# Differential attention: the product with the values between the wide and the narrow scores on TensorE

## What is computed

```
def attend(q, k, v):
    s = einsum('cbhqd,cbhkd->cbhqk', q, k)      # c = 0, 1; d = 64
    p = softmax(s, axis=-1)
    a = p[0] - lam_val * p[1]
    return einsum('bhqk,bhkv->bhqv', a, v)      # v has 128 columns
```

## Time and profile before

| | us |
|---|---|
| three runs, median (lowest, highest) | 4268.17 (4264.69, 4269.55) |
| span of the profiled execution, first to last instruction | 4263.6 |
| PE busy in it | 3903.4 (92%) |
| DVE busy | 2098.1 (49%) |
| ACT busy | 1607.7 (38%) |
| POOL busy | 562.6 (13%) |
| PE share of the chain that ended last | 77% |

### The profile page before, as it was taken

One profiled execution on the slowest core, in us unless ns is written; L12 is line 12 of the kernel. 1 busy time (PEld: TensorE's weight loads), 2 busy tenths in 40 slices (PEclk: granted clock), 3 DMA queues, 4 the chain that ended last, 5 costly groups with the idle time before them and its releaser, 6 DMA issues.

```text
span 4263.6 us, 67437 instructions
## 1 busy us (share of the span) xinstructions
PE 3903.4 (92%) x28266; PEld 3208.1 (75%) x28266; DVE 2098.1 (49%) x3022; ACT 1607.7 (38%) x2639; POOL 562.6 (13%) x628
## 2 busy tenths in 40 slices
PE   6988897878999998988899989999999998899999
PEld 4866686766888776756688766677888887678887
DVE  3545454656221353267523664454655427655564
ACT  3333333333111233155322335644334336554333
POOL 0035303642000001002100000000220003000220
PEclk8988898888999999999899999999999999999999
DMA  5234433131221122101233230131223330322232
GB/s 155 82 130 144 149 97 115 35 100 50 70 70 60 55 71 69 60 11 57 94 98 99 79 85 21 42 129 51 91 97 99 95 108 15 112 79 77 93 103 85
DMA packets 248534, 355.08 MB, mean 83 GB/s; under 512 B 9299, under 2 KB 158502, under 8 KB 247846
## 3 DMA queue, kind: packets, MB, share of 16 engines
q1 hardware_dynamic: 233840, 300.49, 21.9%
q0 software_dynamic: 13840, 50.11, 3.7%
q10 hardware_dynamic: 550, 0.17, 0.0%
HBM read 336.50 MB, written 14.24 MB: 82 GB/s over the span
## 4 chain that ended last, share of the span: by engine, by line
PE 77%; DVE 12%; ACT 7%; issue 2%; POOL 2%; DMA 1%; ACTq 0%; DVEq 0%; SPq 0%; POOLq 0%
PE psum L233 20%; PE psum L234 20%; PE psum L235 20%; PE psum L230 14%; ACT arena L341 3%; DVE arena L264 3%; PE psum L239 3%; DVE arena L274 2%; DVE rw L264 2%; DVE rx L335 2%; ACT arena L345 1%; POOL arena L379 1%; DVE arena L278 1%; ACT rw L345 1%; DVE arena L270 1%
## 5 line engine op out<-in xcount | busy, mean ns | idle before, releaser
L233 PE MATMUL psum<-rx,rw 128*128 128x512 f32 (+2 forms) x2864 | 1047.0, 366 | 54.9 <-DVE rx L335 28.8
L234 PE MATMUL psum<-rx,rw 128*128 128x512 f32 (+2 forms) x2864 | 1028.0, 359 | 0.0
L235 PE MATMUL psum<-rx,rw 128*128 128x512 f32 (+2 forms) x2864 | 1027.1, 359 | 0.0
L264 DVE TENSOR_TENSOR rw<-arena,rw 128x2048 fp32r<-128x2048 f32 (+2 forms) x239 | 537.5, 2249 | 828.8 <-ACT rw L345 822.9
L230 PE MATMUL psum<-arena 32*32 32x32 f32 (+10 forms) x12982 | 802.7, 256 | 148.0 <-ACT arena L345 63.8
L230 PEld LDWEIGHTS psum<-arena 32*32 32x32 f32 (+5 forms) x12982 | 608.7, 140 | 322.5 <-ACT arena L345 102.2
L345 ACT ACTIVATE rw<-arena 128x2048 fp32r<-128x2048 f32 (+2 forms) x239 | 448.1, 1875 | 753.9 <-PE psum L235 730.0
L233 PE MATMUL psum<-rw,rx 128*128 128x512 f32 (+1 forms) x1720 | 681.2, 396 | 45.2 <-DVE rx L335 27.2
L234 PE MATMUL psum<-rw,rx 128*128 128x512 f32 (+1 forms) x1720 | 671.5, 390 | 0.0
L235 PE MATMUL psum<-rw,rx 128*128 128x512 f32 (+1 forms) x1720 | 671.5, 390 | 0.0
L233 PEld LDWEIGHTS psum<-rx,rw 128*128 128x128 f32 (+1 forms) x2864 | 549.2, 192 | 156.4 <-DVE rx L335 42.4
(11 more groups left out here) (71 smaller groups left out, 2091.3 us busy)
## 6 DMA issues: line engine op xcount, KB each, us to landing
arena<-in_ffn_w_up SPq DMA_DIRECT2D x66, 1024.0 KB, 5.1
arena<-in_ada_w SPq DMA_DIRECT2D x48, 1024.0 KB, 5.2
arena<-in_ffn_w_down SPq DMA_DIRECT2D x40, 1024.0 KB, 5.0
arena<-in_ffn_w_gate SPq DMA_DIRECT2D x22, 1024.0 KB, 5.1
arena<-in_dn_w_in SPq DMA_DIRECT2D x32, 512.0 KB, 5.4
arena<-in_xa_w_kv SPq DMA_DIRECT2D x16, 1024.0 KB, 5.1
arena<-in_hgrn_w_in SPq DMA_DIRECT2D x16, 1024.0 KB, 5.5
arena<-in_da_w_in SPq DMA_DIRECT2D x12, 1024.0 KB, 5.2
```

The costliest lines, as they stand in the source:

```text
L233: self.e.matmul(out, l[0], r[0], start=start, stop=False)
L234: self.e.matmul(out, l[0], r[1], start=False, stop=False)
L235: return self.e.matmul(out, l[1], r[0], start=False, stop=stop)
L264: return self.e.tensor_tensor(out, a, b, op)
```

## The change

TensorE's order in a round was: wide scores, narrow scores, product, turns. It becomes: wide scores, product, narrow scores, turns. The same matmuls are issued with the same operands; the wait for `da_e` stays in front of the wide scores, the wait for `da_aT` in front of the product, and the signal `da_s` stays on the narrow scores. The other engines' programs are the same.

```diff
+def pe_da_scores(p, K, i, o, size):
+    QT, KT, VT = da_mem(K)
+    h, qt = da_unit(i)
+    return [p.mm(da_scores(K, i, c)[:, o:o + size], QT[c * 64:c * 64 + 64, h, qt * 128:(qt + 1) * 128],
+                 KT[c * 64:c * 64 + 64, h, o:o + size]) for c in range(2)]
...
@@ pe_da_units
                 prior = divmod(2 * i + c - 3, 2)
                 if prior[0] >= 0:
                     p.wait_ge(*K.at("da_e", *prior))
-            for o, size in ((0, 512), (512, 256)):
-                for c in range(2):
-                    ins = p.mm(da_scores(K, i, c)[:, o:o + size], QT[c * 64:c * 64 + 64, h, qt * 128:(qt + 1) * 128],
-                               KT[c * 64:c * 64 + 64, h, o:o + size])
-                    if o:
-                        ins.then_inc(*p.sig(("da_s", i, c)))
+            pe_da_scores(p, K, i, 0, 512)
         if da_unit(i - 3):
...
                 ins = p.mm(da_product(K), e1[:, c * 128:(c + 1) * 128], VT[:, c, h * 128:(h + 1) * 128], c == 0, c == 5)
             ins.then_inc(*p.sig(("da_o", i - 3)))
+        if da_unit(i):
+            for c, ins in enumerate(pe_da_scores(p, K, i, 512, 256)):
+                ins.then_inc(*p.sig(("da_s", i, c)))
         if da_unit(i - 2):
```

## The result

| | before | changed |
|---|---|---|
| median of 5 runs, us | 4269.55 (4264.69 to 4278.35) | 4361.01 (4356.82 to 4369.32) |
| ratio of the runs, 95% interval | 1 | 1.0214 (1.0202 to 1.0227) |
| profiled execution: time, span | span 4263.6 | 4369.32, span 4367.1 |
| mean granted clock of PE | 0.955 | 0.942 |
| minimum of round 3 to that of round 31 | 128.94 | 218.37 |

The change makes the kernel 91 us slower, where 65 were forecast; the direction and the two causes were right, and the size fell outside the range (4304 to 4356).

The account below looks back on a forecast made before the run. The prediction saw no full engine, only a closed loop of waits of 4.46 us a round. Product and cover (+43) plus clock (+22) gave +65 on 4268, so 4333 us, with the forecast range 4318 to 4352, 4304 to 4356 including rival 1.

Parts of the forecast that it names:

- What bounds the stage: In the stage of 64 DVE minima no engine is full; a closed chain of waits sets 4.46 us a round.
- Product into the loop: DVE's minimum now waits for the product before the narrow scores: 1.62 us a round, 1.44 to 1.70, over 29 rounds.
- The wait for the turned copy: The product's wait on PE for ACT's copy of unit i-3 costs 0, at most 0.05 us a round.
- Cover for the squares: Longer rounds hide DVE's squaring of finished heads in six late rounds, saving 0.67 us each, -4.0 in all.
- The clock falls, because PE waits 2.0 in each round: PE's wait before turns 4 and 5 grows from 0.56 to 2.00 us, repeatedly lowering its clock to 0.8 to 0.85.
- Rival 1: PE's clock stays full throughout the stage: 4311 us, with ends 4306 and 4315; chance 0.19.
- Rival 2: PE's clock is low for three quarters of the stage: 4371 us; chance 0.08 together with all above 4352.
- The clock's price: One third of the stage's time at half speed: +0.77 us a round over 29 rounds, +22; bounds 0 and +28.
- tail: The rounds 32 to 34, which have no scores, keep their times.

Follow-up runs that it names:

- filled kernel: The changed kernel with two extra wide matmuls per round, rounds 3 to 30, in PE's wait between turns 3 and 4; 4317.74 us.
- short version: The changed kernel with only the first of the six blocks of each product, five left out; 4330.35 us.
- copy-first kernel: The changed kernel with ACT's copy of the product moved in front of the exponential of map 0; 4290.17 us.
- changed, one filler: The changed kernel with one extra wide matmul per round in PE's wait; 4320.70 us.
- split, one block between: The changed kernel with one product block between wide and narrow scores and five behind the narrow ones; 4281.84 us.
- split, three blocks between: The changed kernel with three product blocks between wide and narrow scores and three behind the narrow ones; 4297.53 us.
- before, short, one filler: The kernel before with one of six blocks in each product and one extra wide matmul in PE's wait, rounds 3 to 30; 4272.21 us.
- before, short: The kernel before, old order, with only the first of six blocks of each product; 4279.67 us.

## Why the forecast was right in kind and wrong in size

- *What bounds the stage:* right. The chain of the earlier trace rows came back with one piece changed.
- *Product into the loop, 1.62 a round:* measured 6.19 - 4.46 = 1.73, just above my high end of 1.70. Six blocks are 1.33 and the restarts 0.40; my 1.62 left 0.29 for the restarts. Over 29 rounds that is 3 us.
- *The wait for the turned copy, 0:* no round shows it as a piece of the chain. The weight loads are put down to ACT's copy, which ends at 1857.82 + 0.81 = 1858.63, and the first comes at 1858.77, still before the wide records end (1857.72 + 1.13 = 1858.85, with the length of the earlier trace rows); how much of the 0.40 is this and how much the switch between 64-row and 128-row matmuls was not separated and stays open.
- *Cover for the squares, -4:* right. In the filled kernel all rounds take 6.19 or 6.20, square or not.
- *The clock falls, because PE waits 2.0 in each round:* the mechanism is shown. The wait is 1.94, and a change of the wait moves the clock in both orders and both ways (changed order filled: 1.00; old order with a long wait: 0.86, filled again: 0.95). What was changed with it each time is PE's work between two waits; how far the clock follows the one and how far the other stays open. Rival 1 fails: only the filled kernel takes 4318, near its 4311. Rival 2's picture, PE's wait down to 1.56 in slow rounds, fails too: the wait was 1.94 in them, since turns 0 to 3 ran at full clock again (0.66 at 1989.46 and 1997.26); only in the short version, where they ran slow, was it 1.49. By the rule of the Trainium skill's page "TensorE: Matmul & The Clock Gate" (section "Why this matters for your kernels") the clock should have stayed; the runs disagree, 0.77 with waits of 1.94.
- *The clock's price, +22:* this is the step that failed. Measured in the stage: 218.37 - 28 x 6.19 = +45. The failed sentence is the average, "a round is on average 1/(0.6/6.08 + 0.4/9.2)", and the third of the time that went into it. First, the clock was 0.77: 99 of 218 us, 45% of the time, at half speed, not 33%; by my own formula that is 1/(0.55/6.08 + 0.45/9.2) = 7.17, +32. Second, the formula lets low clock fall evenly on work and wait. It does not: PE is busy in 97 of the 99 us, so nearly every microsecond of them costs half a microsecond (45 lost), and that is the other 13. Both of my bounds, +0 and +28, were made with that average, so the range inherited the fault, and 4361 fell between the forecast and rival 2, to which I had given 0.08 together with all above 4352. A bound that would have held needs no average: a round whose work runs wholly at half speed, about 9.2 (the slowest here are 9.24), in all 29 rounds: 29 x (9.2 - 6.08) = +90 on top of the +43, far above 4361.

The sum with the measured terms: 29 x 1.73 - 4 = +46, clock in the stage +45, tail +2 where I had put 0, together 93 against 91.5 between the medians.

## What to carry to other kernels

Work moved within one engine's queue costs its full length when what stands behind it is released later and nothing else covers it: look in the chain of waits for what runs in whose shadow before reordering, and count the restarts. When the move opens a regular wait on TensorE, price its clock by rounds run wholly at half speed and not by a mean, since here the slow time fell on the work behind the wait. If such a wait can't be avoided, matmuls that nobody needs can be worth it, if they end before the wait does.

## What the runs showed of the hardware that was not expected

Adding work made kernels faster: the changed order by 43 us (56 extra wide matmuls) and 40 us (28), the order of before with a short product by 0.2% (28; 8 us in its stage). One filler was as good as two.

PE's wait before turns 4 and 5 (in the copy-first kernel before the scores) and the granted clock of this stage:

| kernel | wait, us | round at full clock, us | clock |
|---|---|---|---|
| before | 0.56 (squares 1.24) | 4.46 | 1.00 |
| changed, two fillers | none | 6.19 | 1.00 |
| changed, one filler | 0.89 | 6.19 | 1.00 |
| split, one block between | 0.78 (squares 0.85) | 5.08 | 1.00 |
| split, three blocks between | 1.23 | 5.52 | 1.00 |
| copy first | 1.26 | 5.36 | 1.00 |
| before, short, one filler | 0.62 (squares 1.31) | 4.46 | 0.95 |
| before, short | 1.67 (squares 2.36) | 4.46 | 0.86 |
| changed | 1.94 | 6.19 | 0.77 |
| changed, short | 1.94, 1.49 | 5.08 (estimate) | 0.61 |

The waits that went with a fall are on the whole the longer ones, but their length does not settle it alone: 1.26 in every round left the clock at 1.00, while four of the six waits of 1.31 in the filled short kernel had a fall behind them, and the same 1.94 went with 0.77 and, with less work between the waits, with 0.61. What else counts was not tested.

From round 17 to round 30 the changed kernel alternated between rounds of 9.24 and 7.80, with a clock of 0.70 over such a pair; its earlier rounds were a mixture of 6.19, 7.8 and 9.2. Why it settled there was not tested.
